# Streaming the experts of a two-block transformer: a third row buffer, four buffers for c, and adds ahead of splits

## The chip, the cores and the metric

The kernel runs on one core of one Trainium2 chip. The metric is the device time of one execution in microseconds (us). Several executions were timed; one more was profiled, and all durations below come from that one.

## The reference, cut to what matters

Two transformer blocks over 256 tokens of width 2048, all in float32: attention of several kinds, a pooling mixer and cross attention, each with its projections, and at the end a PEER layer, which is where the change lies. PEER has 16384 experts, each with a row in `w_u` and a row in `w_v`. A query projection and two tables of 128 sub-keys choose 16 experts for each of 8 heads and token:

```python
def expert_block(args):
    hb, ib, gb = args
    u = jnp.take(w_u, ib, axis=0)
    a = jnp.einsum('td,tkd->tk', hb, u)
    c = gb * jax.nn.gelu(a)
    vv = jnp.take(w_v, ib, axis=0)
    return jnp.einsum('tk,tkd->td', c, vv)
```

The result is added to the residual x, and a last RMS norm with a gain gives the output.

## The kernel before, in words

**Float32 products from parts.** A slab of weights is 1 MB, 128 partitions x 2048 floats. It lands in one of four `raw` buffers; ScalarE (ACT) copies its rounded high part to `w_hi` (line 1402, `split` on ACT), VectorE (DVE) writes the rest, raw minus high, to `w_lo` (line 2153, `split` on DVE), and TensorE (PE) forms each product from high and low parts. The sync engine (SP) loads slab n into buffer n mod 4 as soon as `item_used` says that TensorE has finished item n-4 (lines 649 and 650). Both splits of item m+2 stand in step m of their engines' programs.

**Two ways through PEER.** For the first 192 tokens (SD) every expert's row is multiplied: 128 slabs of `w_u` and 128 of `w_v`, in four parts of 32 items each (QTR = 32). The order is U0, U1, V0, U2, V1, U3, V2, V3. For the last 64 tokens (SG) only the chosen rows are fetched: 64 gathers from `w_u` and then 64 from `w_v`, each an indirect DMA of 128 rows of 8 KB, issued by GpSimd (POOL, line 2132) into one of two buffers, `ROWS`. DVE takes each with one row operation: a dot product with the token's row for `w_u` (line 3008), a scaled addition into `YSUM` for `w_v` (line 3018). Gather n waits on POOL until row operation n-2 is done (`row_used`). How many row operations stand in a part is written by hand in `ROW_SHARE`, spread evenly over its first 30 steps by `take_rows`.

**U items.** TensorE's `activations` (lines 1249 to 1264) puts two sums side by side in one of two PSUM banks, with 16 pairs of matmuls: 384 columns for both parts of h, 192 for the low weights. DVE adds the halves (`add_halves`, line 2991) and TensorE may reuse the bank when that is done (`sums_done`); ACT applies GELU (`activate`, line 1965); DVE multiplies by the gates (`weigh_item`, line 2985). In the first 24 items of U1, TensorE, DVE and ACT also build the gates (`dense`, `hots`, `weigh`, `keep`): `keep` on ACT waits for `weigh` on DVE. DVE's step m in `u_part`, before:

```python
u_split(i, s, q)
if m == QTR - 1:
    low_c(0, 0, q - 1)
add_halves(i, s, q)
```

ACT's step m is the high split of item m+2, at the last step `high(0, 0, ...)` of the V part that follows, then the GELU of item m.

**V items.** c (the weighed activations, 192 tokens) is split too: ACT's `high` writes its high part (line 1999), DVE's `low_c` the rest in two subtractions (lines 2999 and 3000). Two buffers, `c_parts`, hold them, so `high` of item m+1 waits until item m-1 is done. TensorE's `outputs` (lines 1288 to 1315) multiplies both by the slab: 20 matmuls of 512 columns into all eight PSUM banks (lines 1306 to 1312), waiting for `lo_done` and `c_lo_done`. Step m of a V part on DVE is `low_c` of item m+1, the low split of item m+2, then the row operation, if one falls there; on ACT `high` of item m+1, then the high split of item m+2. At the end of V0 and V1 two banks are added into x; at the end of V3 all eight (`bank_ends`, line 3102), and the last norm follows.

**x.** The residual is `x[:, 0]` (tokens 0 to 127) and `x[:, 1]` (128 to 255). From U0 on, POOL has copied the last 64 tokens' part of `x[:, 1]` to `YSUM` and cleared it (lines 2118 to 2121); `x[:, 1]` is not touched again until the last additions.

Of the kernel before, what the change touches and what calls it, by code (L numbers as in the profile page):

```python
# [117 lines left out]
def build_in(nc, A, out, ctx):  # L118
# [17 lines left out]
    c_hi, c_lo = c_parts[:, :, 0:S], c_parts[:, :, S:2 * S]  # L136
    WORK = 24928
    work = sb("work", [P, WORK])
# [69 lines left out]
    pick_in = sem("pick_in")  # L208
    row_in = [sem(f"row_in{b}") for b in range(2)]
    row_used = sem("row_used")  # L210
    row_gelu = sem("row_gelu")
    row_c = sem("row_c")
# [371 lines left out]

    ROWS = [W(22880, D), W(18432, D)]
    HROW, GROW = W(20832, D), W(22880, D)
    YSUM = gaps[:, :, :, SD:S].rearrange("p k n t -> p (k n) t")
    N_U, N_ROWS = P * SG // P, 2 * P * SG // P
    PAIRS = W(20480, 2, P)
    PQT = W(0, KC, S)  # L590
# [158 lines left out]
    def _(pe):  # L749
# [538 lines left out]
        def outputs(i, s, q, first, last):  # L1288
# [6 lines left out]
            for b in banks:  # L1295
                if first and b == 2 and q == 0:
                    pe.wait_ge(kept, 2 + STEPS)
                if first and b == 0 and q <= LASTU:
                    pe.wait_ge(sums_done, 2 + QTR * (q + 1))
                n = b % 4  # L1300
                o = ps[:, b, :]
                wh, wl = w_hi[:, s, n * 512:(n + 1) * 512], w_lo[:, s, n * 512:(n + 1) * 512]
                begins, ends_ = first and b in fresh, last and b in ends
                if b < 4:
                    ch, cl = c_hi[:, s % 2, 0:P], c_lo[:, s % 2, 0:P]
                    pe.matmul(o, ch, wh, start=begins, stop=False, skip_group_check=True)  # L1306
                    pe.matmul(o, ch, wl, start=False, stop=False, skip_group_check=True)  # L1307
                    mm = pe.matmul(o, cl, wh, start=False, stop=ends_, skip_group_check=True)  # L1308
                else:
                    c2 = c_parts[:, s % 2, P:S]  # L1310
# [75 lines left out]
    def _(act):  # L1386
# [604 lines left out]
        def high(i, s, q):  # L1991

            if not isinstance(i, int) or 4 * i + s >= 2 or q > LASTU:
                act.wait_ge(item_used, 4 * i + (v_first[q] + s - 1))
            if q > LASTU and isinstance(i, int) and i + s == 0:
                act.wait_ge(weighed, PIECES + 2 * QTR)
            if q == 0 and isinstance(i, int) and i + s == 0:
                act.wait_ge(gate_used, 2 + STEPS)
            act.activation(c_hi[:, s % 2, 0:SD], CTS[q % 2][:, bass.ds(4 * i + s, 1)].rearrange("p a t -> p (a t)"),
                           ACT.Copy).then_inc(c_hi_done, 1)  # L2000

        def u_part(q):
# [13 lines left out]
            for s in range(RAW):  # L2016
# [96 lines left out]
    def _(pool):  # L2113
# [6 lines left out]
        pool.wait_ge(y_set, 2)  # L2120
        pool.memset(x[SG:P, 1], 0.0).then_inc(y_set, 1)
        pool.wait_ge(picked, 2)
        pool.dma_start(gsm[0:SG, 0], gsm[SG:P, 2]).then_inc(pick_in, 16)
        pool.wait_ge(pick_in, 16)
        for n in range(N_ROWS):
            if n == 1:
                for b in range(2):
                    pool.wait_ge(gates_out[b], 16 + 16 * STEPS // 2)
            if n >= 2:
                pool.wait_ge(row_used, n - 1)  # L2130
            k = n % N_U
# [11 lines left out]
    def _(dve):  # L2143
# [851 lines left out]
        def low_c(i, s, q):  # L2995

            dve.wait_ge(c_hi_done, 4 * i + (c_first[q] + s + 1))
            c = CTS[q % 2][:, 4 * i + s]
            dve.tensor_tensor(c_lo[:, s % 2, 0:P], c[:, 0:P], c_hi[:, s % 2, 0:P].bitcast(F32), ALU.subtract)
            dve.tensor_tensor(c_parts[:, s % 2, SD:S], c[:, P:SD], c_hi[:, s % 2, P:SD].bitcast(F32), ALU.subtract  # L3000
                              ).then_inc(c_lo_done, 1)

        def rows():

            dve.wait_ge(h_in, 16)
            for n in range(N_U):
                dve.wait_ge(row_in[n % 2], 16 * (n // 2 + 1))
                dve.tensor_tensor_reduce(ROWS[n % 2], ROWS[n % 2], HROW, 1.0, 0.0, ALU.mult, ALU.add,  # L3008
                                         AROW[:, n:n + 1]).then_inc(row_used, 1)
# [22 lines left out]
        def weave():  # L3032

            hots(0)
            for m in range(QTR):
                i, s = m // RAW, m % RAW
                if m + 1 < STEPS:
                    hots(m + 1)
                u_split(i, s, 1)
                if m == QTR - 1:  # L3040
                    low_c(0, 0, 0)
                add_halves(i, s, 1)
                if m < STEPS:
                    weigh(i, s)

        def u_part(q):

            dve.wait_ge(gates_in, 16 * PIECES * q)
            for m in range(QTR):
                i, s = m // RAW, m % RAW  # L3050
                u_split(i, s, q)
                if m == QTR - 1:
                    low_c(0, 0, q - 1)
                add_halves(i, s, q)
                if m > 0:
                    weigh_item((m - 1) // RAW, (m - 1) % RAW, q)
# [144 lines left out]
```

## Time and profile before

| | us |
|---|---|
| median of 3 runs | 3046.75 |
| lowest, highest | 3034.57, 3051.47 |
| the profiled execution's own time | 3036.65 |
| its span in the profile | 3034.8 |
| busy: PE, DVE, ACT, POOL | 2817.5, 2133.7, 1345.7, 255.6 |
| mean DMA rate, granted TensorE clock | 227 GB/s, 0.98 |

PE is TensorE's matmuls, PEld its weight loads, DVE is VectorE, ACT ScalarE, POOL GpSimd, SP the sync engine; a q after the name is the engine's queue for DMA. L1306 is line 1306 of the kernel. Where a row has brackets at its end, they say how long the engine had been idle before the instruction and what ended the wait. Matmuls are pipelined and a matmul's length in the trace covers the whole pipeline, so the pitch from one start to the next is what counts. The granted clock is a share of full speed (2.4 GHz); the DMA share is the mean busy share of the core's 16 DMA engines.

### The profile page before, as it was taken

The numbers are of one execution on the slowest core, as the hardware profiler recorded it, in microseconds if no ns is written. First come the engines' busy times: TensorE is split into PE (matmuls) and PEld (weight loads), VectorE is DVE, ScalarE is ACT, GpSimd is POOL, SyncE is SP. The second block draws the span as 40 slices with busy tenths as digits, with TensorE's granted clock in tenths as the row PEclk, the third lists the DMA queues.
The fourth block names the chain that finished last, engine by engine and source line by source line (L and its number), as shares of the span: only waits on it lengthen the run. The fifth ranks groups of instructions, "written<-read, shape, count | busy, mean of one in ns | idle before, by whom it ended". The sixth has DMA issues, their size and how long they took to land.

```text
span 3034.8 us, 39269 instructions
## 1 busy us (share of the span) xinstructions
PE 2817.5 (93%) x15570; PEld 2445.3 (81%) x15570; DVE 2133.7 (70%) x2671; ACT 1345.7 (44%) x1504; POOL 255.6 (8%) x139
## 2 busy tenths in 40 slices
PE   8999989899999999999899999988998889988898
PEld 6888778789887788878799998867898669876775
DVE  4656775656687554565568988678787787878787
ACT  4544454445444443345535544443344444443343
POOL 0000000000000000000000000001122112223331
PEclk9999999899999999999999999999999999999999
DMA  6555535145453555444355556689887998789996
GB/s 243 182 196 181 196 129 182 59 170 180 164 183 120 181 180 187 161 153 173 136 179 180 194 207 212 220 321 357 343 319 291 374 346 306 309 312 343 343 345 243
DMA packets 112774, 690.24 MB, mean 227 GB/s; under 512 B 12873, under 2 KB 25921, under 8 KB 34385
## 3 DMA queue, kind: packets, MB, share of 16 engines
q1 hardware_dynamic: 73152, 522.03, 47.8%
q0 software_dynamic: 18544, 134.78, 11.5%
q10 hardware_dynamic: 20960, 31.84, 3.0%
q8 instruction: 77, 1.26, 0.2%
q14 instruction: 41, 0.33, 0.0%
HBM read 675.40 MB, written 12.58 MB: 227 GB/s over the span
## 4 chain that ended last, share of the span: by engine, by line
PE 53%; DVE 23%; DMA 11%; ACT 8%; issue 3%; ACTq 2%; DVEq 0%; SPq 0%
DVE w_lo L2153 10%; PE ps L796 9%; PE ps L798 9%; PE ps L797 9%; ACT w_hi L1402 6%; DMA raw<-in_w_v 5%; PE ps L854 3%; DMA work<-in_w_v,gsm 3%; PE ps L856 3%; PE ps L855 3%; DVE gaps L3018 2%; DVE work L3008 2%; DMA work<-in_w_u_rows,gsm 2%; PE ps L1306 2%; PE ps L1308 2%
## 5 line engine op out<-in xcount | busy, mean ns | idle before, releaser
L2153 DVE TENSOR_TENSOR w_lo<-raw,w_hi 128x2048 fp32r<-128x2048 f32 (+2 forms) x500 | 1129.1, 2263 | 507.9 <-ACT w_hi L1402 501.2
L1402 ACT ACTIVATE w_hi<-raw 128x2048 fp32r<-128x2048 f32 (+2 forms) x500 | 942.1, 1891 | 615.4 <-DMA raw<-in_w_v 239.2
L796 PE MATMUL ps<-w_hi,hT 128*128 128x512 f32 (+3 forms) x1344 | 519.3, 386 | 11.6 <-DVE w_lo L2153 11.1
L798 PE MATMUL ps<-w_hi,hT 128*128 128x512 f32 (+3 forms) x1344 | 512.2, 381 | 0.0
L797 PE MATMUL ps<-w_lo,hT 128*128 128x512 f32 (+3 forms) x1344 | 511.9, 381 | 0.0
L1258 PE MATMUL ps<-hT,w_hi 128*128 128x384 f32 x1536 | 419.7, 354 | 29.6 <-DVE work L2991 29.1
L1306 PE MATMUL ps<-w_hi,c_parts 128*128 128x512 f32 x512 | 215.8, 421 | 91.8 <-DVE c_parts L3000 86.5
L796 PEld LDWEIGHTS ps<-w_hi,hT 128*128 128x128 f32 x1344 | 253.4, 189 | 59.1 <-DVE w_lo L2153 8.6
L798 PEld LDWEIGHTS ps<-w_hi,hT 128*128 128x128 f32 x1344 | 253.2, 188 | 45.5
L797 PEld LDWEIGHTS ps<-w_lo,hT 128*128 128x128 f32 x1344 | 253.5, 189 | 44.0
L1261 PEld LDWEIGHTS ps<-hT,w_lo 128*128 128x128 f32 x1536 | 278.8, 188 | 0.0
L1261 PE MATMUL ps<-hT,w_lo 128*128 128x192 f32 x1536 | 278.5, 263 | 0.0
L1258 PEld LDWEIGHTS ps<-hT,w_hi 128*128 128x128 f32 x1536 | 233.5, 192 | 43.1 <-DVE work L2991 42.1
L1306 PEld LDWEIGHTS ps<-w_hi,c_parts 128*128 128x128 f32 x512 | 100.8, 197 | 138.3 <-DVE c_parts L3000 84.0
L1307 PE MATMUL ps<-w_lo,c_parts 128*128 128x512 f32 x512 | 208.6, 407 | 0.0
L1308 PE MATMUL ps<-w_hi,c_parts 128*128 128x512 f32 x512 | 208.4, 407 | 0.0
L1311 PE MATMUL ps<-w_hi,c_parts 128*128 128x512 f32 x512 | 202.5, 396 | 0.1
L1312 PE MATMUL ps<-w_lo,c_parts 128*128 128x512 f32 x512 | 201.2, 393 | 0.0
L2132 POOL DMA_INDIRECT work<-in_w_v,gsm x64 | 152.4, 2382 | 359.9 <-DVE gaps L3018 350.7
L3018 DVE SCALAR_TENSOR_TENSOR gaps<-work,gsm,gaps 128x2048 f32<-128x2048 f32 x64 | 150.3, 2348 | 29.3 <-DMA work<-in_w_v,gsm 29.2
L854 PE MATMUL ps<-w_hi,hT 128*128 128x512 f32 x384 | 153.2, 399 | 11.2 <-DVE hT L2256 11.0
L1965 ACT ACTIVATE work<-work (+1 forms) x96 | 35.0, 364 | 289.1 <-DVE work L2991 289.1
(302 smaller groups left out, 4202.6 us busy)
## 6 DMA issues: line engine op xcount, KB each, us to landing
raw<-in_w_u_t SPq DMA_DIRECT2D x128, 1024.0 KB, 4.8
raw<-in_w_v SPq DMA_DIRECT2D x128, 1024.0 KB, 7.4
raw<-in_w_in_2.0 SPq DMA_DIRECT2D x32, 1024.0 KB, 4.7
raw<-in_odd_w.0 SPq DMA_DIRECT2D x20, 1024.0 KB, 4.9
raw<-in_even_w.3608 SPq DMA_DIRECT2D x16, 1024.0 KB, 4.9
raw<-in_w_out.0 SPq DMA_DIRECT2D x16, 1024.0 KB, 4.9
raw<-in_w_out.1 SPq DMA_DIRECT2D x16, 1024.0 KB, 4.8
raw<-in_w_out_2.0 SPq DMA_DIRECT2D x16, 1024.0 KB, 4.8
```

The lines of the kernel that those rows point to most:

```text
L796: pe.matmul(o, hi, wh, start=(j + k == 0), stop=False)
L797: pe.matmul(o, hi, wl, start=False, stop=False)
L798: mm = pe.matmul(o, lo, wh, start=False, stop=(j == 3 and k == 3))
L854: pe.matmul(o, hi, wh, start=begins and k == 0, stop=False)
L1258: pe.matmul(both_parts, w_hi[:, s, k * P:(k + 1) * P], hT[:, k, :, 0:SD], start=(k == 0), stop=False, skip_group_check=True)
L1261: mm = pe.matmul(ps[:, s % 2, 0:SD], w_lo[:, s, k * P:(k + 1) * P], hT_hi[:, k, 0:SD], start=False, stop=(k == KC - 1), skip_group_check=True)
L1306: pe.matmul(o, ch, wh, start=begins, stop=False, skip_group_check=True)
L1307: pe.matmul(o, ch, wl, start=False, stop=False, skip_group_check=True)
L1308: mm = pe.matmul(o, cl, wh, start=False, stop=ends_, skip_group_check=True)
L1402: act.activation(w_hi[:, s, 0:size], raw[:, s, 0:size], ACT.Copy).then_inc(hi_done, 1)
L2153: dve.tensor_tensor(w_lo[:, s, 0:size], raw[:, s, 0:size], w_hi[:, s, 0:size].bitcast(F32), ALU.subtract).then_inc(lo_done, 1)
L3018: dve.scalar_tensor_tensor(out=YSUM, in0=ROWS[n % 2].rearrange("p (a t) -> p a t", t=SG), scalar=CROW[:, n - N_U:n - N_U + 1], in1=YSUM, o ...
```

## The change

It is five edits that share their buffers.

- A third buffer for gathered rows, `x[:, 1]`. POOL first copies `x[:, 1]` to a tensor in HBM (`x_kept`), and back when row operation 126 of 128 is done; the last additions on DVE wait for that (`x_back`). Gather n now waits for row operation n-3.
- Four buffers for c's parts: two more, `c_more` in the place of the two masks that attention used, and `c_hole` in the work area. `high` and `low_c` run two items ahead, and `high` of item m+2 waits for item m-2.
- At the end of a U part the c of two items is prepared for the V part that follows.
- On DVE `add_halves` of item m comes ahead of the low split of item m+2, in `weave` (U1) and `u_part` (U2, U3); `low_c` ahead of both.
- Row operations by part, before: V0 24, U2 16, V1 24, U3 16, V2 26, V3 22; after: 22, 20, 22, 20, 22, 22.

Of the diff, in this order: the buffers, ACT's `high`, `u_part` and `v_step`, POOL, and DVE's row shares, `u_part` (`weave` changes likewise), `v_step` and end.

```diff
-    ROWS = [W(22880, D), W(18432, D)]
+    ROWS = [W(22912, D), W(18432, D), x[:, 1]]
+    C = [c_parts[:, 0], c_parts[:, 1], c_more, c_hole]
...
         def high(i, s, q):
 
-            if not isinstance(i, int) or 4 * i + s >= 2 or q > LASTU:
-                act.wait_ge(item_used, 4 * i + (v_first[q] + s - 1))
+            if not isinstance(i, int) or 4 * i + s >= 4 or q > LASTU:
+                act.wait_ge(item_used, 4 * i + (v_first[q] + s - 3))
...
                 if q > 0 and s == RAW - 1:
                     high(0, 0, q - 1)
+                    high(0, 1, q - 1)
...
             def v_step(i, s, last=False):
-                if not (last and s == 3):
-                    high(i + (s + 1) // 4, (s + 1) % 4, q)
+                if not (last and s >= 2):
+                    high(i + (s + 2) // 4, (s + 2) % 4, q)
                 elif q == LASTU:
-                    high(0, 0, q + 1)
+                    high(0, s - 2, q + 1)
...
         pool.memset(x[SG:P, 1], 0.0).then_inc(y_set, 1)
+        pool.wait_ge(y_set, 3)
+        pool.dma_start(x_kept, x[:, 1]).then_inc(x_away, 16)
...
-            if n >= 2:
-                pool.wait_ge(row_used, n - 1)
+            if n == 2:
+                pool.wait_ge(x_away, 16)
+            if n >= 3:
+                pool.wait_ge(row_used, n - 2)
...
+        pool.wait_ge(row_used, N_ROWS - 2)
+        pool.dma_start(x[:, 1], x_kept).then_inc(x_back, 16)
...
-        ROW_SHARE = {("V", 0): 24, ("U", 2): 16, ("V", 1): 24, ("U", 3): 16, ("V", 2): 26, ("V", 3): 22}
+        ROW_SHARE = {("V", 0): 22, ("U", 2): 20, ("V", 1): 22, ("U", 3): 20, ("V", 2): 22, ("V", 3): 22}
...
                 i, s = m // RAW, m % RAW
-                u_split(i, s, q)
                 if m == QTR - 1:
                     low_c(0, 0, q - 1)
+                    low_c(0, 1, q - 1)
                 add_halves(i, s, q)
+                u_split(i, s, q)
...
             def v_step(i, s, last=False):
-                if not (last and s == 3):
-                    low_c(i + (s + 1) // 4, (s + 1) % 4, q)
+                if not (last and s >= 2):
+                    low_c(i + (s + 2) // 4, (s + 2) % 4, q)
                 elif q == LASTU:
-                    low_c(0, 0, q + 1)
+                    low_c(0, s - 2, q + 1)
...
-        dve.wait_ge(y_set, 3)
+        dve.wait_ge(x_back, 16)
         for n, b in enumerate(END_BANKS):
             bank_ends(b).then_inc(fin_add, 1)
```

## Rows read from the trace of the kernel before

**Rows 1.** Windows of six stages: span, busy us PE PEld DVE ACT POOL, PEclk, DMA, GB/s:
```profile
1985.73:2162.04 176.31, 157.88 (x641) 124.68 (x642) 145.02 (x153) 71.36 (x64) 24.37 (x24) 0.95 0.93 359
2162.04:2328.25 166.21, 153.04 (x1024) 148.45 (x1024) 131.08 (x129) 70.11 (x64) 43.29 (x16) 1.00 0.81 309
2328.25:2505.21 176.96, 157.94 (x641) 124.59 (x642) 138.56 (x147) 71.61 (x65) 24.23 (x24) 0.95 0.91 346
2505.21:2670.76 165.55, 152.54 (x1025) 148.34 (x1024) 132.06 (x114) 70.11 (x64) 43.10 (x16) 0.99 0.81 309
2670.76:2845.00 174.24, 152.23 (x623) 120.72 (x624) 139.67 (x122) 69.89 (x65) 60.10 (x26) 0.96 0.91 335
2845.00:3020.28 175.28, 158.46 (x660) 125.41 (x659) 136.30 (x125) 71.75 (x68) 48.12 (x22) 0.97 0.85 313
```

**Rows 2.** Waits, total, times, longest: two of V2, then one of V3:
```profile
PE ps L1306 <- DVE c_parts L3000: 27.3, 15, 5.3
DVE gaps L3018 <- DMA work<-in_w_v,gsm: 20.2, 14, 2.3
...
PE ps L1306 <- DVE c_parts L3000: 16.7, 10, 4.6
```

**Rows 3.** One stall of V2, timelines of POOL, DVE, PE: start, us, instruction [idle before]:
```profile
2690.18 3.09 POOL L2132 DMA_INDIRECT work<-in_w_v,gsm  x1 [4.33 <-DVE gaps L3018]
...
2700.59 2.35 DVE L3018 SCALAR_TENSOR_TENSOR gaps<-work,gsm,gaps 128x2048 f32<-128x2048 f32 x1 [2.11 <-DMA work<-in_w_v,gsm]
...
2703.33 0.79 PE L1306 MATMUL ps<-w_hi,c_parts 128*128 128x512 f32 x1 [2.82 <-DVE c_parts L3000]
...
2707.12 0.39 PE L1307 MATMUL ps<-w_lo,c_parts 128*128 128x512 f32 x1
...
2713.70 0.39 PE L1312 MATMUL ps<-w_lo,c_parts 128*128 128x512 f32 x1
```

**Rows 4.** One round of U3, timelines of DVE, ACT and PE:
```profile
2541.22 0.55 DVE L2991 TENSOR_REDUCE work<-ps 128x192 f32<-128x384 f32 x1
...
2544.12 2.29 DVE L2153 TENSOR_TENSOR w_lo<-raw,w_hi 128x2048 fp32r<-128x2048 f32 x1 [2.08 <-ACT w_hi L1402]
2546.33 0.55 DVE L2991 TENSOR_REDUCE work<-ps 128x192 f32<-128x384 f32 x1
...
2541.92 0.36 ACT L1965 ACTIVATE work<-work  x1 [3.02 <-DVE work L2991]
2542.19 1.90 ACT L1402 ACTIVATE w_hi<-raw 128x2048 fp32r<-128x2048 f32 x1
...
2515.34 0.54 PE L1258 MATMUL ps<-hT,w_hi 128*128 128x384 f32 x2
...
2541.14 0.54 PE L1258 MATMUL ps<-hT,w_hi 128*128 128x384 f32 x2
```

**Rows 5.** Waits in 22 dense rounds of U1 (1800 to 1948 us):
```profile
DVE w_lo L2153 <- ACT w_hi L1402: 21.3, 22, 3.6
...
PE ps L1258 <- DVE work L2991: 12.3, 19, 1.9
```

**Rows 6.** The passage from U3 to V2, timelines of DVE and PE:
```profile
2667.99 2.29 DVE L2153 TENSOR_TENSOR w_lo<-raw,w_hi 128x2048 fp32r<-128x2048 f32 x1 [1.96 <-ACT w_hi L1402]
...
2670.76 0.77 PE L1306 MATMUL ps<-w_hi,c_parts 128*128 128x512 f32 x1 [5.32 <-DVE c_parts L3000]
```

**Rows 7.** The busiest 20 us of V0 for the DMA engines, columns as rows 1:
```profile
2120.00:2140.00 20.00, 17.95 (x77) 13.92 (x75) 15.37 (x15) 7.55 (x7) 1.87 (x2) 1.00 1.01 409
```

**Rows 8.** Landing of one slab of weights in V0, line 650:
```profile
DMA to landing us min/median/max: 5.7/8.2/11.3
```

**Rows 9.** The kernel's end on DVE, and the copy of x among DMA issues:
```profile
2998.82 2.35 DVE L3018 SCALAR_TENSOR_TENSOR gaps<-work,gsm,gaps 128x2048 f32<-128x2048 f32 x1
...
3016.27 4.88 DVE L3102 TENSOR_TENSOR x<-x,ps 128x512 f32<-128x512 f32 x8 [0.95 <-PE ps L1312]
...
x<-in_x SPq DMA_DIRECT2D x2, 1024.0 KB, 13.4
```

More of the change, by code:

```diff
@@ L136, in build_in @@
     c_hi, c_lo = c_parts[:, :, 0:S], c_parts[:, :, S:2 * S]
-    WORK = 24928
+    WORK = 24960
     work = sb("work", [P, WORK])
@@ L208, in build_in @@
     pick_in = sem("pick_in")
-    row_in = [sem(f"row_in{b}") for b in range(2)]
+    row_in = [sem(f"row_in{b}") for b in range(3)]
     row_used = sem("row_used")
+    x_away = sem("x_away")
+    x_back = sem("x_back")
     row_gelu = sem("row_gelu")
@@ L583, in build_in @@
     gates_kept = nc.dram_tensor("gates_kept", (P, KEPT, STEPS, QTR * TG), F32, kind="Internal").ap()
-    ROWS = [W(22880, D), W(18432, D)]
-    HROW, GROW = W(20832, D), W(22880, D)
+    ROWS = [W(22912, D), W(18432, D), x[:, 1]]
+    HROW, GROW = W(20864, D), W(22912, D)
+    x_kept = nc.dram_tensor("x_kept", (P, D), F32, kind="Internal").ap()
     YSUM = gaps[:, :, :, SD:S].rearrange("p k n t -> p (k n) t")
     N_U, N_ROWS = P * SG // P, 2 * P * SG // P
-    PAIRS = W(20480, 2, P)
+    PAIRS = W(12288, 2, P)
     PQT = W(0, KC, S)
@@ L613, in build_in @@
     gsm = sb("gsm", [P, 4, P])
+    c_more = nc.alloc_sbuf_tensor_at("c_more", [P, 2 * S], F32R, offset=RAW_AT + 4 * (2 * RAW * 2048 + 4 * S + WORK + P + P // 2))
+    c_hole = nc.alloc_sbuf_tensor_at("c_hole", [P, 2 * SD], F32R, offset=RAW_AT + 4 * (2 * RAW * 2048 + 4 * S + 20480))
+    C = [c_parts[:, 0], c_parts[:, 1], c_more, c_hole]
     IOTA = gsm[:, 3]
@@ L1304, in outputs @@
                 if b < 4:
-                    ch, cl = c_hi[:, s % 2, 0:P], c_lo[:, s % 2, 0:P]
+                    ch, cl = C[s][:, 0:P], C[s][:, S:S + P]
                     pe.matmul(o, ch, wh, start=begins, stop=False, skip_group_check=True)
@@ L1309, in outputs @@
                 else:
-                    c2 = c_parts[:, s % 2, P:S]
+                    c2 = C[s][:, P:S]
                     pe.matmul(o, c2, wh, start=begins, stop=False, skip_group_check=True)
@@ L2998, in low_c @@
             c = CTS[q % 2][:, 4 * i + s]
-            dve.tensor_tensor(c_lo[:, s % 2, 0:P], c[:, 0:P], c_hi[:, s % 2, 0:P].bitcast(F32), ALU.subtract)
-            dve.tensor_tensor(c_parts[:, s % 2, SD:S], c[:, P:SD], c_hi[:, s % 2, P:SD].bitcast(F32), ALU.subtract
+            dve.tensor_tensor(C[s][:, S:S + P], c[:, 0:P], C[s][:, 0:P].bitcast(F32), ALU.subtract)
+            dve.tensor_tensor(C[s][:, SD:S], c[:, P:SD], C[s][:, P:SD].bitcast(F32), ALU.subtract
                               ).then_inc(c_lo_done, 1)
@@ L3006, in rows @@
             for n in range(N_U):
-                dve.wait_ge(row_in[n % 2], 16 * (n // 2 + 1))
-                dve.tensor_tensor_reduce(ROWS[n % 2], ROWS[n % 2], HROW, 1.0, 0.0, ALU.mult, ALU.add,
+                dve.wait_ge(row_in[n % 3], 16 * (n // 3 + 1))
+                dve.tensor_tensor_reduce(ROWS[n % 3], ROWS[n % 3], HROW, 1.0, 0.0, ALU.mult, ALU.add,
                                          AROW[:, n:n + 1]).then_inc(row_used, 1)
@@ L3015, in rows @@
             for n in range(N_U, N_ROWS):
-                dve.wait_ge(row_in[n % 2], 16 * (n // 2 + 1))
+                dve.wait_ge(row_in[n % 3], 16 * (n // 3 + 1))
                 dve.wait_ge(row_used, n)
-                dve.scalar_tensor_tensor(out=YSUM, in0=ROWS[n % 2].rearrange("p (a t) -> p a t", t=SG),
+                dve.scalar_tensor_tensor(out=YSUM, in0=ROWS[n % 3].rearrange("p (a t) -> p a t", t=SG),
                                          scalar=CROW[:, n - N_U:n - N_U + 1], in1=YSUM, op0=ALU.mult, op1=ALU.add
@@ L3038, in weave @@
                     hots(m + 1)
-                u_split(i, s, 1)
                 if m == QTR - 1:
                     low_c(0, 0, 0)
+                    low_c(0, 1, 0)
                 add_halves(i, s, 1)
+                u_split(i, s, 1)
                 if m < STEPS:
```

6 lines of the change are left out of this document (3 added, 3 removed).

## The prediction, made before the result was known

> **What bounds the kernel now.** I read the page's busy shares by slice first: everything the diff touches lies in the last third, where experts' rows are streamed. The six stages V0, U2, V1, U3, V2 and V3 fill 1985.7 to 3020.3 us, 1034.6 us in all [rows 1]. In them no engine is full: TensorE shows 152 to 158 us busy per stage, but its matmuls overlap, so I take its floor from their pitch. Without a stall 29 matmuls of V start in 6.58 us [rows 3], 0.227 each; an item of 20 needs 4.54 us and 32 items 145; the V stages take 174 to 177, with a mean granted clock of 0.95 to 0.97 (some at 1.2 GHz, most at 2.4) against 0.99 to 1.00 in U. In U, 45 pairs of 384-column matmuls start in 25.80 us [rows 4]; at 0.573 us a pair an item (8 pairs and their low halves) needs 4.59 us and a stage 147, against 160 of the 166 (the rest is the gap at the end, below). The DMA engines are the closest to full: 0.93, 0.91, 0.91 and 0.85 in V, 0.81 in U. Share times length, summed over the six rows, is 901 us: no order of the work gets these bytes through sooner unless the engines move faster than they do now.
>
> Three loops make up the difference. **V:** the waits say that TensorE waits for DVE's low part of c, 15 times in V2 and 10 in V3, and that DVE's row operation waited 14 times in V2 for a gather [rows 2]. The timeline shows the link: a gather issued at 2690.18 lands only at 2700.59, and with two buffers it could be issued only when the operation two before its own had ended; DVE stands 2.11 us, works 2.35, and the low part queued behind it lets TensorE start 2.82 us late [rows 3]. V3, with 22 rows, stalls too: there late weights and a row operation together hold the low part back. **U:** add at 2541.22, GELU at 2541.92, the high split at 2542.19, the low split at 2544.12, next add at 2546.33 [rows 4]: each step waits for the one before, 5.11 us a round, because DVE puts the next split ahead of the add that releases ScalarE. TensorE's 4.59 us isn't what paces it. **Passage:** from U to V TensorE stands 5.32 us, as the low part of the first c sits behind a split that waited 1.96 us [rows 6]; there are three such passages.
>
> **The change, part by part.**
>
> *Third row buffer.* A gather now has three row operations' time, not two. By the stall above, one turn of a buffer is 10.4 us of flight, 2.35 of work and some 0.3 of hand-over: 13 us, shared by two rows 6.5, by three 4.4. V2 needed 26 rows in 174 us, 6.7 us apart, so two buffers were its pace; 22 rows over three buffers need 96 us and are off the path. One more gather can be in flight, so weights' landing (8.2 us median, 11.3 at most in V0 [rows 8]) gets company; this is the forecast's weak point.
>
> *Four c buffers, one item more ahead.* The low part no longer stands behind the last row operation and split before it is needed. On ScalarE high(m+2) now waits for item m-2, which also releases the slab that the split right behind it waits for; so the new wait blocks nothing that could have run. No operation is added. It gives the V stages the length of one row operation, 2.35 us, as slack.
>
> *Add ahead of split.* The add now stands for the end of item m with split, weighing and row operation queued behind it. Item m+2 needs that split: after the item's end come add 0.55 and split 2.29, 2.84 us, against an item of 4.59. DVE was busy 131 us in U2 with 16 row operations [rows 1], 4.1 an item; four more make 4.4, just under 4.59. An item with a row operation is 5.3 and one without 2.9, so at two in three it carries over at most 1.4 us, and the split still ends in time. So the round is broken and TensorE or the DMA engines pace U. In U1's dense rounds, too, DVE stood for the high split, 21.3 us in 22 rounds, and TensorE 12.3 us for the add [rows 5]. A round there took 6.73 us, 6.2 without TensorE's idle. ScalarE's copy of the gates waits for the weighing, which now comes after the split, so a loop stays, and no row shows its length. I take 11 us, nearest to TensorE's idle; the ends are 0 (the later weighing costs what the earlier add gives) and 15 (all of TensorE's idle, with adds the trace lacks). Its last eight plain items gain 8 x 0.5 = 4 us.
>
> *Low parts of two c's ahead of the add* at a stage's end. They still follow ScalarE's split, but that no longer waits for a late add; 5.3 us shrinks to about 0.5. For U2 and U3 this lies inside the stage times; for U1 it is 4.8 us more. The second pair of subtractions, 0.5 us on DVE, is moved, not added.
>
> *Shares 22 and 20.* A gather is 128 rows of 8 KB, 1.05 MB. V0 and V1 lose 2.1 MB each, V2 4.2, V3 none; U2 and U3 gain 4.2.
>
> *x put away and brought back.* The copy out goes on POOL's queue in U0, where POOL stands idle until the first gathers; nothing waits, cost 0. Were that cover gone, gather 2 alone would be late by the copy's flight. The copy back is issued after the third-last row operation, and every last addition now waits for it. Before, that operation ended at 3001.17 and the additions began at 3016.27 [rows 9]: 15 us, some 12 with quicker items. No such copy is in the trace; the nearest is x's load, 13.4 us with two at once [rows 9], and in V0 a slab of that size takes 5.7 to 11.3 [rows 8]. So 0 to 8 us late; I take 1, as the last weights land meanwhile.
>
> **The sum.** In each stage the DMA work is share x length, scaled by the bytes (GB/s x length, so 63.3 MB in V0) [rows 1], and I let it run at a share of 0.94: above V0's 0.93, the best whole stage, since the stalls that left engines without work are gone, and below the 1.0 of its best 20 us [rows 7]. V0 164.0 x 61.2/63.3 / 0.94 = 168.6; U2 134.6 x 55.6/51.4 / 0.94 = 154.9; V1 165.5; U3 154.4; V2 158.6 x 54.2/58.4 / 0.94 = 156.6; V3, with 1 MB of x more, 161.5. Together 961.5, against 1034.6: 73.1 us less. All stay above TensorE's 145 and 147. With U1's 11 + 4 + 4.8 and 1 lost at the end, 92 us less. The profiled execution took 3036.65 (span 3034.8), which gives 2945; it lies 10 us under the median shown, 3046.75, near the fastest of the three. I add 3 of the 10 and forecast **2948 us**.
>
> The six stages then move some 341 MB in 961.5 us, 355 GB/s; now the best stage holds 359, and the best 20 us held 409 [rows 1, 7]. The Trainium skill ("DMA: Bandwidth & Descriptors", section "Where 436 GB/s comes from") says that for transfers between HBM and SBUF a limit of about 358 GB/s per core binds. By that rule the stages can't fall below 954 us nor the time below some 2937; the 409 of this trace, on one core, speaks against it as a hard limit.
>
> **The rivals.**
> *The DMA engines don't fill further.* A mean of 340 GB/s, between V1's 346 and V2's 335 [rows 1], is what two queues give when slabs and gathers delay each other: waits for c turn into waits for weights. For it: V3, with fewer gathers, stalled as well [rows 2]. Against: V0's 20 us at 409 [rows 7]. 341/0.340 = 1004 us, 31 less, with U1's and the end 2987. The limit that the Trainium skill states (above) would point here, as the forecast leaves no margin to it.
> *Nothing left but TensorE and a full DMA.* At a share of 1.00: 158.5 + 155.5 + 147.2 + 151.8 and 147 twice is 907; 2890 with the rest. For it: the 1.0 of V0's 20 us; against: no whole stage came near. The Trainium skill's limit would exclude it.
> *Weights come too late, slower.* Place: line 650's slabs, behind up to three gathers. Slab n loads when item n-4 ends and is needed three items later; flight, high split 1.9, low split 2.3, a row operation 2.35 ahead of it and the item itself make four items, so an item takes (flight + 11.1)/4: 4.8 us at V0's median of 8.2, 5.5, the pace of now, at 10.9. For a loss of 0.5% it must also eat U's and U1's gains, 57 us over 128 items: 5.94, flight 12.6, above any seen [rows 8]. At 13 the V stages take 771 and the kernel 3064.
> *No change:* the rows moved into U make DVE, at 4.4 us of 4.59, miss its turn, giving back there what V wins; it needs both U stages 46 us longer than forecast, which no row suggests; 3037.
>
> **How the numbers follow.** A measurement of this kernel tells about 0.5% from no change, 15 us. Forecast 0.61, DMA not filling further 0.21, the floors 0.10, no change 0.05, slower 0.03. The first three are all faster: 0.92; same 0.05, slower 0.03. The forecast alone spans 2915 (share 0.97) to 2976 (0.91). Down to 2900 the range takes in half of the floors' case, whose 2890 rises where U1 gains less than 11 or the copy back costs up to 8; up to 2995 it takes in most of the DMA case, 2987 and those same bounds. What is left out is under 2 in 10.
>
> **What would show it.** Right: waits of row operations for gathers nearly gone; TensorE's wait for the low part of c gone or replaced by one for w_lo; adds in U following the end of the item, items of 4.6 to 4.8 us, and no gap of 5 us before a V stage; DMA share 0.92 to 0.97 in all six stages. Wrong: slabs landing at a median above 10 us in V, U items still at 5.1, or the last additions waiting for the copy of x.

## The result, and the profile after

The changed kernel takes 2914.12 us (median of four runs, 2907.92 to 2920.7) against 3041.24 us (median of four, 3034.57 to 3051.47) before: a ratio of 0.9591, 95% interval 0.9571 to 0.9612. It is faster by 4.1%; 2948 had been forecast, with 2900 to 2995 as the range. The profiled execution took 2914.41 us, its span is 2912.6.

Lines of the changed kernel have moved by 6 to 15: TensorE's matmuls are L1264 and L1267 (U) and L1312 to L1318 (V), the low split is L2166, the high one L1408, the add L3004, the weighing L2998, c's high part L2005 and low part L3012 and L3013, the row operations L3021 and L3031, the gathers L2143, the slabs' loads L656, the last additions L3117. Busy time, share of the span and instructions of each engine, first line of the profile's page:

```profile
PE 2781.1 (95%) x15570; PEld 2423.3 (83%) x15570; DVE 2129.5 (73%) x2671; ACT 1340.1 (46%) x1504; POOL 204.9 (7%) x141
```

The work is the same; the time between went. Windows of the six stages V0, U2, V1, U3, V2, V3 (columns as in [rows 1]; V0's and V1's end with their last matmul, 1.1 and 1.5 us ahead of the first one of U2 and U3):

```profile
1971.53:2131.20 159.67, 150.99 (x642) 118.33 (x640) 138.95 (x146) 69.25 (x63) 27.64 (x22) 1.00 0.98 386
2131.20:2284.71 153.51, 148.52 (x1025) 147.22 (x1025) 139.58 (x139) 72.01 (x65) 22.88 (x21) 1.00 0.94 358
2284.71:2438.05 153.34, 149.48 (x640) 118.79 (x640) 132.75 (x142) 67.29 (x62) 22.37 (x22) 1.00 0.97 389
2438.05:2591.41 153.36, 148.42 (x1024) 147.35 (x1025) 141.43 (x120) 73.92 (x67) 22.52 (x20) 1.00 0.94 356
2591.41:2744.00 152.59, 150.36 (x640) 120.03 (x640) 132.08 (x121) 67.74 (x64) 47.72 (x22) 0.99 0.93 366
2744.00:2897.70 153.70, 149.60 (x642) 119.14 (x642) 134.73 (x122) 68.76 (x64) 47.20 (x21) 1.00 0.91 355
```

Beside [rows 1] each stage is shorter, by 12 to 24 us, and together they take 926.2 us against 1034.6. The DMA share rose most in U (0.81 to 0.94) and V3 (0.85 to 0.91), and the granted clock of V from between 0.95 and 0.97 to between 0.99 and 1.00. Where the span's 122.2 us came from, by the first matmul of each stage:

| | before | after | difference | forecast |
|---|---|---|---|---|
| start to U1 | 1773.57 | 1778.04 | +4.5 | 0 |
| U1 | 212.2 | 193.5 | -18.7 | -19.8 |
| six stages | 1034.6 | 926.2 | -108.4 | -73.1 |
| the rest, after the last matmul of V3 | 14.5 | 14.9 | +0.4 | +1 |

The first matmul of U1, before and then after:

```profile
1773.57 0.61 PE L1258 MATMUL ps<-hT,w_hi 128*128 128x384 f32 x2 [0.43 <-issue]
...
1778.04 0.61 PE L1264 MATMUL ps<-hT,w_hi 128*128 128x384 f32 x2 [0.43 <-issue]
```

The expectations of two runs below give 1779.8 us for the changed kernel, a lag of 6.2, and 1779.7 for the third buffer alone. The traces have matmuls of U1 from 1778.04 and from 1776.56 us on: the changed kernel's lag is 4.5 us.

TensorE's waits (total, times, longest), first in V0 to V1, then in V2 and V3:

```profile
PE ps L1312 <- DVE w_lo L2166: 12.4, 18, 1.4
PE ps L1264 <- DVE w_lo L2166: 2.7, 7, 0.6
PE ps L1312 <- DVE c_parts L3013: 1.2, 1, 1.2
...
PE ps L1312 <- DVE w_lo L2166: 5.4, 8, 1.3
PE ps L1312 <- DVE c_parts L3013: 1.8, 1, 1.8
```

The waits for the low part of c, 27.3 us in V2 and 16.7 in V3 [rows 2], are down to the one at the passage, 1.8. A wait for the low weights has come in their place, 5.4 us in both stages. The row operation's wait for a gather [rows 2] is gone: the page's group of them (those from the two old buffers) shows no idle time ahead at all (last column), and no group of row operations has any:

```profile
L3031 DVE SCALAR_TENSOR_TENSOR gaps<-work,gsm,gaps 128x2048 f32<-128x2048 f32 x43 | 100.9, 2347 | 0.0
```

Two rounds of U3 on DVE, then ACT, the place of [rows 4]:

```profile
2476.58 0.56 DVE L3004 TENSOR_REDUCE work<-ps 128x192 f32<-128x384 f32 x1 [0.40 <-PE ps L1267]
2477.06 2.28 DVE L2166 TENSOR_TENSOR w_lo<-raw,w_hi 128x2048 fp32r<-128x2048 f32 x1
2479.26 0.35 DVE L2998 TENSOR_TENSOR work<-work 128x192 f32<-128x192 f32 x1
2479.53 2.35 DVE L3031 SCALAR_TENSOR_TENSOR gaps<-x,gsm,gaps 128x2048 f32<-128x2048 f32 x1
2481.79 0.55 DVE L3004 TENSOR_REDUCE work<-ps 128x192 f32<-128x384 f32 x1
...
2477.28 0.36 ACT L1971 ACTIVATE work<-work  x1 [1.25 <-DVE work L3004]
2480.18 1.92 ACT L1408 ACTIVATE w_hi<-raw 128x2048 fp32r<-128x2048 f32 x1 [2.53 <-DMA raw<-in_w_u_t]
```

The add now waits for TensorE (L1267), ScalarE's split for the slab's landing, and DVE's split for nobody; the loop of [rows 4] is open. Two rows of DVE follow here back to back, 5.21 us an item, and DVE catches up in the items without a row: the stage's mean is 153.36 / 32 = 4.79 us. The passage from U3 to V2, which cost 5.32 us [rows 6], on TensorE, and the end on DVE and POOL beside [rows 9]:

```profile
2591.41 0.47 PE L1312 MATMUL ps<-w_hi,c_parts 128*128 128x512 f32 x1 [1.77 <-DVE c_parts L3013]
...
2885.04 0.58 POOL L2147 DMA_DIRECT2D x<-x_kept  x1 [5.05 <-DVE gaps L3031]
...
2892.00 2.35 DVE L3031 SCALAR_TENSOR_TENSOR gaps<-work,gsm,gaps 128x2048 f32<-128x2048 f32 x1
2894.26 4.86 DVE L3117 TENSOR_TENSOR x<-x,ps 128x512 f32<-128x512 f32 x8
```

The copy back is issued 9.2 us ahead of the last additions, and those follow the last row operation without a gap: its wait costs nothing. Last, the landing of a slab in V0, beside [rows 8]:

```profile
DMA to landing us min/median/max: 5.5/9.5/12.2
```

The median went from 8.2 to 9.5 us: slabs do have more company, and an item of V0 still takes 159.67 / 32 = 4.99 us, against 5.51 before.

### The profile page after: what moved, and what is told of

It is laid out like the page before. It is cut to its first block, busy times and chain, and to the rows that moved or that the text cites. A ratio compares the mean times of both kernels' runs of the same rounds, so it can differ in the third digit from the quotient of the medians.

```text
span 2912.6 us, 39271 instructions
## 1 busy us (share of the span) xinstructions
PE 2781.1 (95%) x15570; PEld 2423.3 (83%) x15570; DVE 2129.5 (73%) x2671; ACT 1340.1 (46%) x1504; POOL 204.9 (7%) x141
## 4 chain that ended last, share of the span: by engine, by line
PE 66%; DVE 17%; DMA 8%; ACT 6%; ACTq 2%; issue 2%; DVEq 0%; SPq 0%
PE ps L802 9%; PE ps L804 9%; PE ps L803 9%; DVE w_lo L2166 9%; DMA raw<-in_w_v 5%; PE ps L1264 5%; ACT w_hi L1408 4%; PE ps L860 3%; PE ps L862 3%; PE ps L861 3%; PE ps L1267 3%; PE ps L1312 3%; PE ps L1318 2%; PE ps L1314 2%; PE ps L1317 2%; PE ps L1313 2%
## 5 line engine op out<-in xcount | busy, mean ns | idle before, releaser
L2166 DVE TENSOR_TENSOR w_lo<-raw,w_hi 128x2048 fp32r<-128x2048 f32 (+2 forms) x500 | 1128.3, 2261 | 422.5 <-ACT w_hi L1408 416.0
L1408 ACT ACTIVATE w_hi<-raw 128x2048 fp32r<-128x2048 f32 (+2 forms) x500 | 943.3, 1893 | 777.6 <-DMA raw<-in_w_v 325.6
L1264 PE MATMUL ps<-hT,w_hi 128*128 128x384 f32 x1536 | 415.4, 352 | 11.6 <-DVE w_lo L2166 8.3
L1267 PEld LDWEIGHTS ps<-hT,w_lo 128*128 128x128 f32 x1536 | 278.1, 188 | 0.0
L1267 PE MATMUL ps<-hT,w_lo 128*128 128x192 f32 x1536 | 277.9, 262 | 0.0
L1264 PEld LDWEIGHTS ps<-hT,w_hi 128*128 128x128 f32 x1536 | 233.1, 192 | 17.1 <-issue 16.9
L860 PE MATMUL ps<-w_hi,hT 128*128 128x512 f32 x384 | 153.8, 400 | 12.7 <-DVE hT L2269 12.4
L862 PE MATMUL ps<-w_hi,hT 128*128 128x512 f32 x384 | 151.1, 394 | 0.0
L861 PE MATMUL ps<-w_lo,hT 128*128 128x512 f32 x384 | 151.1, 394 | 0.0
L1275 PE MATMUL ps<-hT,w_hi 128*128 128x192 f32 x512 | 140.5, 274 | 2.4 <-DVEq L701 1.1
L1276 PE MATMUL ps<-hT,w_hi 128*128 128x192 f32 x512 | 140.2, 274 | 0.0
L1277 PE MATMUL ps<-hT,w_lo 128*128 128x192 f32 x512 | 140.2, 274 | 0.0
L1312 PE MATMUL ps<-w_hi,c_parts 128*128 128x512 f32 x256 | 103.7, 405 | 9.7 <-DVE w_lo L2166 6.3
L3031 DVE SCALAR_TENSOR_TENSOR gaps<-work,gsm,gaps 128x2048 f32<-128x2048 f32 x43 | 100.9, 2347 | 0.0
L1275 PEld LDWEIGHTS ps<-hT,w_hi 128*128 128x128 f32 x512 | 98.3, 192 | 3.1 <-issue 1.6
```

Of the source, the lines that this page charges most:

```text
L860: pe.matmul(o, hi, wh, start=begins and k == 0, stop=False)
L861: pe.matmul(o, hi, wl, start=False, stop=False)
L862: mm = pe.matmul(o, lo, wh, start=False, stop=ends and k == 3)
L1264: pe.matmul(both_parts, w_hi[:, s, k * P:(k + 1) * P], hT[:, k, :, 0:SD], start=(k == 0), stop=False, skip_group_check=True)
L1267: mm = pe.matmul(ps[:, s % 2, 0:SD], w_lo[:, s, k * P:(k + 1) * P], hT_hi[:, k, 0:SD], start=False, stop=(k == KC - 1), skip_group_check=True)
L1275: pe.matmul(o, wh, hT_hi[:, k, 0:SD], start=(k == 0), stop=False)
```

## The experiments

Nine kernels were run: four take one edit back, one does one edit alone, one leaves the gathers out, two ask about the lag ahead of U1, one tries to win more. Times are medians of four or five runs; ratios are to the kernel before, whose own median was 3037.0 to 3041.24 us from one set of runs to the next, so a few us between two medians say nothing. Stage lengths come from one profiled execution each, from first matmul to first matmul, V2 and V3 together; in the changed kernel V0 160.7, U2 152.4, V1 154.8, U3 151.8, V2 and V3 306.3, U1 193.5.

**Two row buffers again**

```diff
-    ROWS = [W(22912, D), W(18432, D), x[:, 1]]
+    ROWS = [W(22912, D), W(18432, D)]
...
-        pool.dma_start(x_kept, x[:, 1]).then_inc(x_away, 16)
...
-            if n >= 3:
-                pool.wait_ge(row_used, n - 2)
+            if n >= 2:
+                pool.wait_ge(row_used, n - 1)
...
```

> The changed kernel with two buffers for gathered rows again and no copy of x; all else as changed. Theory (the gather's turn through two buffers paced V): a turn is 13 us, two buffers give a row every 6.5 us, so 22 rows need 143 us of a stage of 153 and each late gather stops DVE; the V stages go from 153-160 to about 165 us, U (20 rows, 130 us) stays, the kernel takes about 2955 us, and row operations wait for gathers again. Rival (the c buffers' slack alone took the stalls away, the third buffer is idle luxury): at most 10 us more, under 2925.

2951.15 us, ratio 0.971 (0.9678 to 0.9743). V0 167.8, V1 162.7, V2 and V3 330.3, U 151.3 and 153.9. So the third buffer is worth 37 us in this company, 39 of them in V. Waits in V2 and V3, of DVE, then of TensorE:

```profile
DVE gaps L3025 <- DMA work<-in_w_v,gsm: 43.7, 20, 5.4
...
PE ps L1312 <- DVE w_lo L2160: 27.8, 15, 5.0
PE ps L1312 <- DVE c_parts L3007: 1.0, 1, 1.0
```

The row operation waits for its gather as before. What TensorE misses now is not c, which has been made two items ahead, but the low weights, whose split stands behind that row operation: a stall in DVE's order is handed to whatever stands next. By the prediction's turn of 13 us two buffers would carry 22 rows in 143 us, less than a stage; 20 gathers were late all the same, by up to 5.4 us each.

**Two c buffers, one item ahead**

```diff
-    C = [c_parts[:, 0], c_parts[:, 1], c_more, c_hole]
+    C = [c_parts[:, 0], c_parts[:, 1]] * 2
...
-                act.wait_ge(item_used, 4 * i + (v_first[q] + s - 3))
+                act.wait_ge(item_used, 4 * i + (v_first[q] + s - 1))
...
-                    high(i + (s + 2) // 4, (s + 2) % 4, q)
+                    high(i + (s + 1) // 4, (s + 1) % 4, q)
...
```

(`low_c` likewise, and one c instead of two at the end of a U part.)

> The changed kernel with two buffers for c's parts, prepared one item ahead, as before; three row buffers, order and shares as changed. Theory (low part of c queued behind a row operation and a late split): TensorE waits for the low part of c again, some 8 us a V stage more by the lost 2.35 us of slack at each late slab, about 2945 us. Rival (the third row buffer alone cures V): at most 8 us more in all, and hardly a wait for c.

2962.84 us, ratio 0.9749 (0.971 to 0.9787): V0 168.7, V1 170.3, V2 and V3 330.4; U2 and U3 are 150.6 and 153.2. The four buffers are worth 49 us, more than was expected of them. TensorE's wait for c in V2 and V3, then one of these waits on ACT, DVE and PE:

```profile
PE ps L1312 <- DVE c_parts L3012: 26.3, 18, 4.0
...
2678.12 1.92 ACT L1408 ACTIVATE w_hi<-raw 128x2048 fp32r<-128x2048 f32 x1 [4.21 <-DMA raw<-in_w_v]
...
2680.07 2.29 DVE L2165 TENSOR_TENSOR w_lo<-raw,w_hi 128x2048 fp32r<-128x2048 f32 x1 [4.10 <-ACT w_hi L1408]
2682.28 2.35 DVE L3030 SCALAR_TENSOR_TENSOR gaps<-x,gsm,gaps 128x2048 f32<-128x2048 f32 x1
...
2685.02 0.50 PE L1312 MATMUL ps<-w_hi,c_parts 128*128 128x512 f32 x1 [2.18 <-DVE c_parts L3012]
```

With three row buffers and no late gather, TensorE still waits 26.3 us for c. The rows say why: a slab lands late, so ScalarE's high split of it and then DVE's low split start late, a row operation follows, and the low part of c, needed next, stands behind both. In the six stages TensorE waits 40 times for c; 37 times the low part follows a row operation without a gap, and in 36 of these ScalarE's split had waited for a slab's landing. This is the theory's mechanism at a higher price, 49 us instead of 31. ScalarE's `high` also waits for the item before last in this run, 51.1 us in V2 and V3; in the stall shown it does not, and c's high part is ready at 2680.3.

**The split ahead of the add again**

```diff
+                u_split(i, s, q)
                 if m == QTR - 1:
                     low_c(0, 0, q - 1)
                     low_c(0, 1, q - 1)
                 add_halves(i, s, q)
-                u_split(i, s, q)
```

(`weave` likewise. The split comes ahead of the two low parts at a stage's end, too.)

> The changed kernel with DVE's low split ahead of the add of halves again; buffers and shares as changed. Theory (the round add, GELU, high split, low split paces U): U items go back to about 5.1 us, U2 and U3 from 153.5 to some 164 us each, U1 some 15 us longer, V unchanged; about 2952 us. Rival (with 20 rows U is paced by the DMA engines, share 0.94, so the order matters little there): U2 and U3 within 3 us of the changed kernel, only U1 slower, about 2930 us.

2964.89 us, ratio 0.9754 (0.9726 to 0.9783). U1 is back at 212.3, U2 and U3 at 166.2 and 168.0; V0 163.6, V1 157.7, V2 and V3 311.4. Windows of U2 and U3 (as [rows 1]), then the largest sum of waits of U3:

```profile
2154.70:2320.88 166.18, 153.18 (x1024) 148.74 (x1025) 140.73 (x138) 70.30 (x65) 54.36 (x20) 1.00 0.87 336
...
2478.58:2646.58 168.00, 153.61 (x1024) 148.84 (x1025) 142.12 (x119) 70.26 (x66) 54.18 (x20) 0.99 0.85 330
...
ACT work L1971 <- DVE work L3004: 92.6, 31, 3.3
```

The place of the split is worth 51 us by the medians. In the profiled execution, which lies 10 us above its median, U1 takes 19 us more than in the changed kernel, near the prediction's step; U2 and U3 together take 30 more, where 21 were expected, and V 11, where none were.

**The old shares**

```diff
-        ROW_SHARE = {("V", 0): 22, ("U", 2): 20, ("V", 1): 22, ("U", 3): 20, ("V", 2): 22, ("V", 3): 22}
+        ROW_SHARE = {("V", 0): 24, ("U", 2): 16, ("V", 1): 24, ("U", 3): 16, ("V", 2): 26, ("V", 3): 22}
```

> The changed kernel with the shares of rows of before (24, 16, 24, 16, 26, 22). Theory (the DMA engines pace V now, at a share of 0.91 to 0.98): two rows more cost V0 and V1 2.1 MB each at 390 GB/s, 5 us each, four more cost V2 11 us; U2 and U3 give 4 to 6 us each back, as they fall to TensorE's 147: net some 10 us more, about 2925 us. Rival (the shares are the change's main part, without them V2 falls back to its old 174 us): 25 us more or over, 2940 or above. Rival 2 (no stage is paced by the DMA engines): within 4 us.

2917.75 us, ratio 0.9598 (0.957 to 0.9626): not to be told from the changed kernel. By stages it moved the way the theory said, V0 +4.3, V1 +1.0 (5 had been expected), V2 and V3 +8.9, U2 and U3 -4.6 each: 14 us more in V against 9 less in U, for eight rows moved. The first four rows of its windows, V0 to U3:

```profile
1971.42:2136.41 164.99, 150.84 (x642) 118.46 (x641) 144.59 (x153) 69.03 (x63) 29.55 (x24) 1.00 0.98 387
2136.41:2284.30 147.89, 147.48 (x1024) 147.01 (x1025) 130.18 (x129) 72.28 (x65) 16.93 (x16) 1.00 0.92 339
2284.30:2440.17 155.87, 150.23 (x641) 118.50 (x641) 138.26 (x147) 68.37 (x63) 28.19 (x24) 1.00 0.99 400
2440.17:2587.46 147.29, 147.01 (x1024) 146.86 (x1025) 131.62 (x114) 73.85 (x67) 17.19 (x16) 1.00 0.92 339
```

With 16 rows U2 takes 147.89 us, the 147 that the prediction gave as TensorE's floor.

**No gathers**

```diff
             k = n % N_U
+            if n >= 3:
+                continue
             pool.indirect_dma_start(
...
```

> The changed kernel without 125 of its 128 gathers (the row operations run on the first three buffers' content, scaled to zero, so the last 64 tokens' part is left out; all row operations stay on DVE). Theory (what holds the V stages at 153 to 161 us and U at 152 is the DMA engines, slabs and gathers sharing them): V stages at 146 to 147 us, U at 147, so some 45 us less, about 2869 us, slabs landing in 5 to 6 us. Rival (DVE, with 4.2 us of work in a V item of 4.54, paces): V stages stay at 152 or more, within 12 us of the changed kernel.

2865.89 us, ratio 0.9429 (0.9403 to 0.9455). Windows of V0, U2, V1, U3 and of V2 with V3:

```profile
1974.14:2122.38 148.24, 146.63 (x643) 119.59 (x641) 139.22 (x148) 69.06 (x63) 0.00 (x0) 1.00 0.78 270
2122.38:2268.04 145.66, 145.31 (x1025) 145.16 (x1025) 138.44 (x137) 70.32 (x65) 0.00 (x0) 1.00 0.63 231
2268.04:2413.24 145.20, 145.20 (x640) 120.19 (x641) 134.64 (x144) 69.30 (x64) 0.00 (x0) 1.00 0.74 253
2413.24:2560.49 147.25, 146.96 (x1026) 146.82 (x1024) 138.09 (x118) 70.30 (x65) 0.00 (x0) 1.00 0.64 228
2560.49:2850.91 290.42, 290.42 (x1281) 240.48 (x1282) 266.35 (x243) 137.10 (x130) 1.33 (x2) 1.00 0.67 228
```

DVE does as much as before (139 us of V0's), and TensorE runs through, 145.2 us in V1 and in each of V2 and V3. So 877 of the changed kernel's 926 us in the six stages are left without gathers, nearly all of it TensorE's pace; the other 49 come with the gathers. Slabs land sooner without them: V1's from `w_v` in a median of 5.4 us here, 8.9 in the changed kernel. DVE's own work, with its row operations, costs nothing as long as no slab and no row is late.

**The third row buffer alone, in the kernel before**

```diff
-    ROWS = [W(22880, D), W(18432, D)]
+    ROWS = [W(22912, D), W(18432, D), x[:, 1]]
...
-            if n >= 2:
-                pool.wait_ge(row_used, n - 1)
+            if n == 2:
+                pool.wait_ge(x_away, 16)
+            if n >= 3:
+                pool.wait_ge(row_used, n - 2)
```

> The kernel before with the third row buffer and the copies of x alone; two c buffers, split ahead of add, old shares. Theory (gather's turn and late low part are two causes that add up; undone singly they cost V 41 and 49 us of 83): the V stages together fall by about 34 us, U1, U2 and U3 stay, 6 us are lost ahead of U1: about 3010 us. Rival (with the low part still behind the row operation, a third buffer cures nothing by itself): within 8 us of before.

3019.16 us, ratio 0.9928 (0.9902 to 0.9953). V0 173.0, V1 171.8, V2 and V3 332.8: 25 us less in V, less than expected, and the total moved by 21. Waits of TensorE in V2 and V3:

```profile
PE ps L1312 <- DVE c_parts L3012: 31.1, 22, 5.3
```

Late gathers were one of two reasons for the wait for c, 44.0 us before [rows 2]; 31.1 stay, near the 26.3 of the run with two c buffers. Neither buffer does the work of the other. Alone the third buffer gives 21 us, in the company of the other edits 37.

**The copies of x: through old tensors, and none**

```diff
-        pool.dma_start(x_kept, x[:, 1]).then_inc(x_away, 16)
+        pool.dma_start(mk_kept, x[:, 1, 0:1024].rearrange("p (a s) -> p a s", a=4)).then_inc(x_away, 16)
+        pool.dma_start(mv_kept, x[:, 1, 1024:2048].rearrange("p (a s) -> p a s", a=NT)).then_inc(x_away, 16)
```

> The changed kernel with x[:, 1] put away in two HBM tensors that the kernel already has and no longer needs then (mk_kept and mv_kept), so no new tensor, two copies of half the size each way. Theory (the profile of every kernel with the new tensor x_kept reaches U1 6.2 us later than before, the one without it at the same time as before, and the lag begins in the first 30 us: the new tensor shifts where the others lie in HBM, and static loads suffer): U1 starts at 1773.6 us again, about 2908 us. Rival (the lag has another cause, such as the third semaphore, the longer POOL program or the copies themselves): U1 starts at 1779.8 as in the changed kernel, 2914 us.

2911.59 us, ratio 0.9583 (0.9559 to 0.9606); U1 begins at 1781.7. The theory fell: the new tensor in HBM is not what delays U1.

```diff
-        pool.dma_start(x_kept, x[:, 1]).then_inc(x_away, 16)
...
-        pool.wait_ge(row_used, N_ROWS - 2)
-        pool.dma_start(x[:, 1], x_kept).then_inc(x_back, 16)
...
-        dve.wait_ge(x_back, 16)
+        dve.wait_ge(row_used, N_ROWS)
```

> The changed kernel without the two copies of x[:, 1] (put away, brought back) and their semaphores; the third row buffer stays. The last 64 experts' rows then overwrite the second tile's residual, which the last additions add in as it stands: the residual of tokens 128 to 255 is left out of the result. It asks where the 6.2 us ahead of U1 come from: U1 starts at 1779.8 us in the changed kernel, at 1779.7 with the third buffer and copies alone, at 1781.7 with the copies through old tensors, but at 1773.6 in the kernel before and with two row buffers and no copies. Theory (the copies, or their two instructions, do it): U1 starts at 1773 to 1774.5, the stages from U1 on stay within 3 us of the changed kernel's 1118, and the time is 2905 to 2910 us. Rival (it is the third buffer, or nothing of the two): U1 starts at 1779 to 1782 and the time is 2912 to 2916 us. For the copy back: if it cost anything at the end, the stretch from the last matmul to the end of the span shrinks by more than 0.5 us.

2911.49 us, ratio 0.9586 (0.9556 to 0.9616); U1 begins at 1779.0. This theory fell too: the copies cost nothing that these runs can tell, at either end (the stretch after the last matmul is 15.8 us against 14.9), and the lag is not theirs. Part of it arises in the first 30 us, long before any of the edits runs. Windows from 15 us on, of the kernel before and then of the changed one:

```profile
15.00:20.00 5.00, 1.82 (x8) 1.38 (x8) 4.33 (x8) 5.00 (x9) 0.00 (x0) 1.00 1.02 422
20.00:25.00 5.00, 4.78 (x14) 3.87 (x15) 5.00 (x7) 2.81 (x2) 0.00 (x0) 0.66 1.01 425
```

```profile
15.00:20.00 5.00, 1.41 (x8) 1.01 (x8) 4.32 (x7) 5.00 (x10) 0.00 (x0) 0.89 1.02 420
20.00:25.00 5.00, 4.61 (x11) 3.67 (x12) 5.00 (x7) 2.97 (x2) 0.00 (x0) 0.50 1.01 425
```

In the second window 11 matmuls are done in place of 14, at 1.2 GHz (0.50) all through instead of for part of it (0.66). The nine kernels with a third row buffer do 6 to 12 matmuls in that window and begin U1 at 1776.6 to 1781.7 us; the two with two buffers (the kernel before, and the run with two row buffers) do 14 and begin it at 1773.6. Each time stands on one profile, and those with three buffers differ by 5 us among themselves. Why a buffer that no gather of the changed kernel reaches before 1944 us should be felt there is open.

**Rows into the end of U1**

V0, at 160.7 us, is the longest stage, and U1 ahead of it has DMA engines to spare (a share of 0.76 over its last eight items). On top of the kernel with x in old tensors, five of V0's row operations go into U1's last steps:

```diff
-        ROW_SHARE = {("V", 0): 22,
+        ROW_SHARE = {("V", 0): 17,
...
                 if m < STEPS:
                     weigh(i, s)
+                if m in (24, 27, 28, 29, 30):
+                    next(rowing)
```

> A version made to beat the changed kernel: x put away in the old tensors as in e6, and five of V0's 22 row operations moved into U1's last eight plain items (steps 24 and 27 to 30), where the DMA engines are a third idle and DVE needs 2.9 us of an item of 4.59. Theory (V0 is paced by the DMA engines, share 0.98, 386 GB/s): 5.2 MB less is 13 us less DMA work, V0 falls from 160.7 to about 149, U1 grows by 0 to 3 us, so 8 to 12 us less than e6, about 2899 us. Rival (the gathers of U1's end can't be in flight early enough, since two of three buffers are free only after the gates are out; DVE stands for them and U1 grows by what V0 wins): within 3 us of e6.

2909.82 us, ratio 0.957 (0.9545 to 0.9595): not to be told from the changed kernel. V0 fell from 162.7 to 156.1, but U1 grew from 193.5 to 197.0. DVE at U1's end, and TensorE's first matmul of V0:

```profile
1969.61 2.29 DVE L3022 CUSTOM_DVE_ANT_0 work<-work 128x2048 f32<-128x2048 f32 x1
...
1972.29 2.28 DVE L2167 TENSOR_TENSOR w_lo<-raw,w_hi 128x2048 fp32r<-128x2048 f32 x1
1974.49 2.29 DVE L3022 CUSTOM_DVE_ANT_0 work<-work 128x2048 f32<-128x2048 f32 x1
...
1976.70 0.29 DVE L3013 TENSOR_TENSOR c_parts<-work,c_parts 128x128 fp32r<-128x128 f32 x1
...
1977.23 0.77 PE L1311 MATMUL ps<-w_hi,c_parts 128*128 128x512 f32 x1 [2.58 <-issue]
```

The last steps, each with a row, take DVE 4.88 us against items of 4.6; it arrives late at the passage, and TensorE stands 2.58 us. Of the 6.6 us won in V0, U1 gives back 3.5, and what is left can't be told from no gain.

## Why the prediction was right, point by point

**The bound on the time.** The forecast's model was DMA work (share times length, 901 us before) at a share of 0.94. The share came out right: over the six rows after, share times length is 875.5 us in 926.2, a share of 0.945. The mis-sized term is the work itself, which the prediction took for a constant ("no order of the work gets these bytes through sooner"). Some 341 MB were 901 us before and 875.5 after: 378 GB/s at full share, then 390. At 378 and the share of 0.945 the six stages would have taken an estimated 955 us, near the forecast's 961.5; by this accounting the term is most of the 35 us by which they beat it.

That the mean share came out right is in part luck. By stage it is 0.91 to 0.98, with two stages outside the 0.92 to 0.97 named as a sign; U2 and U3 came within 1.4 us of the sum, V0, V1 and V3 fell 8 to 12 us below it, and five of the six stages took nearly the same 153 us at shares from 0.91 to 0.97. So no run shows that work over a share sets a stage's length; what the runs do show is that the gathers' presence costs 49 us.

Full share has no fixed rate. In V0 the 20 busiest microseconds before gave 409 GB/s at 1.01 [rows 7]; the changed kernel moves 424 for 45 us at the same share:

```profile
2086.00:2131.00 45.00, 41.14 (x173) 31.39 (x171) 36.72 (x40) 18.83 (x16) 7.83 (x7) 1.00 1.01 424
```

Without gathers the five rows above give 604 us of work for 210 MB, 348 GB/s at full share. So bytes per unit of busy share are no constant. Between the kernels they changed only in V. GB/s over share gives 386, 380, 368 and 368 in V0 to V3 before [rows 1] and 394, 401, 394 and 390 after; U2 and U3 have 381 and 381, then 381 and 379. Why they rose there was not measured.

The Trainium skill's limit ("DMA: Bandwidth & Descriptors", section "Where 436 GB/s comes from") had been set beside the sum: 358 GB/s per core, by which the stages' length was estimated at 954 us or more. They took 926.2, two whole stages ran at 386 and 389 GB/s, and the limit did not bind here. Another page of the Trainium skill ("HBM Reference", section "Specifications (TRN2)") says that a core streaming alone gets about 425 GB/s, bounded by its DMA engines; with the 424 of this trace it agrees.

**The third row buffer:** right. Waits of row operations for gathers are gone, and it is worth 37 us. **Four c buffers:** right in what they do: by the run with two of them the low part does stand behind the last row operation and split. They are worth 49 us, and in the sum they had no price of their own, only "the length of one row operation" as slack. **Stalls and the clock.** The sum left out that TensorE ran slower after a stall: the first matmul after the one of [rows 3] took 0.79 us against 0.39 later, and the granted clock was 0.50 (1.2 GHz) from 2703.33 to 2706.05 us and 1.00 from 2707. With the stalls shorter, V's mean granted clock rose from between 0.95 and 0.97 to between 0.99 and 1.00.

**Add ahead of split:** right. U1 gave 18.7 us of a forecast 19.8, and by parts as well: the dense rounds, from the first matmul of U1 to that of its 25th item (1937.28 us before, 1931.32 after), 10.4 of 11; the last eight items 3.2 of 4; the passage 5.1 of 4.8 (its gap of 5.08 us to the first matmul of V0 is gone). U2 and U3 take 152.4 and 151.8 us against a forecast 154.9 and 154.4; DVE's lateness of two rows in a row is carried and caught up, as reckoned. Of the passages, U3 to V2 keeps 1.77 us instead of 0.5.

**Shares:** the forecast moved the bytes rightly and gave them hardly a price in the end; taking them back cost 4 us, not clear of noise. **Copies of x:** 0, where 1 was taken. **Ahead of U1** 4.5 us were lost that no step had.

**The rivals.** "The DMA engines don't fill further" (2987) fell: no stage is under 0.91, and the mean rate is 368 GB/s against its 340. "Weights too late" (3064) is there in its mechanism and not in its size: landing rose to 9.5 us and TensorE's waits for the low weights in V items from one of 5.1 us at a passage to 18 of 12.4 us in all, V0 to V1; but to make the kernel slower than before it needed a flight of 12.6 us. "No change" needed U stages 46 us longer than forecast; the four rows more cost each stage 4.6 us, by the run with the old shares. "Nothing left but TensorE and a full DMA" (2890) was nearer in its number than the forecast, 24 us away against 34, but not by its mechanism: the share was 0.945, not 1.00. Together the undone edits cost 37 + 49 + 51 + 4 = 141 us and the change gained 127: an edit is worth somewhat more in the others' company than alone, as the third buffer shows, 37 against 21.

## What to carry to other kernels

When no engine is full, look for the loops: an instruction that stands ahead of the one that releases the engine it will itself wait for (add and split here, 51 us for the place of the split), a buffer whose round trip is the pace (the rows), and a small product that is finished only just before its use, behind work that may be late (c). A DMA engine's busy share times length is no floor: beside it, read the rate at the best full stretch, and take stage floors from the compute engines too. Undo each edit by itself; stages that trade gain for gain, as the shares did, show nothing in the total.

## What had not been expected of the hardware

At a busy share of about 1.0 the engines moved 409 or 424 GB/s, and 348 per full share when slabs went alone: the share says how long they were busy, not how much passed. And a third row buffer, reached by a gather only near the end of U1, goes with a start that is slower from the first 30 us, 11 matmuls instead of 14 between 20 and 25 us, and with 4.5 us lost by U1 in the changed kernel (3.0 to 8.1 in all nine); neither the new HBM tensor nor the copies cause it, it stands on one profile of each kernel, and the cause stays open.
